# Turning the FFN product in 32x32 blocks on VectorE and through a DRAM buffer, instead of on TensorE

## The reference

```python
def swiglu(h, w_gate, w_up, w_down):          # h [256, 1024]
    return (jax.nn.silu(h @ w_gate) * (h @ w_up)) @ w_down   # w_gate, w_up [1024, 2816], w_down [2816, 1024]

x = x + 0.5 * swiglu(rms_norm(x, g[0]), ...)   # four times in the first two layers
x = x + (silu(gate) * up) @ w_down             # once in the hybrid layer
```

## Time and profile before

| | |
|---|---|
| time, median of 3 runs | 1378.87 us (1378.53 to 1378.92) |
| time of the profiled execution | 1378.48 us |
| its span, first to last instruction | 1376.7 us |
| PE busy | 1341.6 us (97% of the span) |
| DVE busy | 796.8 us (58%) |
| ACT busy | 645.7 us (47%) |
| POOL busy | 82.2 us (6%) |
| moved by DMA | 233.32 MB, mean 169 GB/s |
| granted clock of TensorE, mean | 0.996 of full |

### The profile page before, as it was taken

How to read it: one execution, slowest core, us unless ns; L and a number is a source line. 1 busy time by engine, 2 the same in 40 slices (tenths; PEclk the granted TensorE clock), 3 DMA queues, 4 the chain that set the end, 5 groups by cost and what they waited for, 6 DMA issues and landing times.

```text
span 1376.7 us, 17712 instructions
## 1 busy us (share of the span) xinstructions
PE 1341.6 (97%) x6710; PEld 1114.1 (81%) x6710; DVE 796.8 (58%) x873; ACT 645.7 (47%) x742; POOL 82.2 (6%) x181
## 2 busy tenths in 40 slices
PE   8999999999999999999999999999999998999998
PEld 7888889877888887788888877888887986788886
DVE  5555459746545545654556876544556887555444
ACT  5444457324444445544444856444445655444442
POOL 2000003100000001200000300000001200000000
PEclk9999999999999999999999999999999999999999
DMA  8655555414655554455553514655543452565551
GB/s 256 218 190 183 183 168 184 153 62 150 219 190 194 186 183 153 155 190 191 192 188 113 193 61 160 201 185 191 191 164 138 156 184 63 175 204 183 183 191 54
DMA packets 159326, 233.32 MB, mean 169 GB/s; under 512 B 7608, under 2 KB 126542, under 8 KB 159278
## 3 DMA queue, kind: packets, MB, share of 16 engines
q1 hardware_dynamic: 156560, 229.17, 50.5%
q10 hardware_dynamic: 2238, 2.70, 0.6%
q0 software_dynamic: 480, 0.80, 0.4%
HBM read 231.58 MB, written 1.05 MB: 169 GB/s over the span
## 4 chain that ended last, share of the span: by engine, by line
PE 92%; DVE 4%; ACT 2%; issue 1%; DMA 0%; POOL 0%; ACTq 0%; DVEq 0%; POOLq 0%
PE ps L250 27%; PE ps L252 26%; PE ps L251 26%; PE ps L545 2%; DVE wl L222 1%; PE ps L1012 1%; PE ps L266 1%; PE ps L334 1%; PE ps L268 1%; PE ps L267 1%; DVE htl L367 1%; PE ps L1526 1%; PE ps L1525 1%; ACT wh L211 1%; ACT hth L354 0%
## 5 line engine op out<-in xcount | busy, mean ns | idle before, releaser
L250 PE MATMUL ps<-wl,hth 128*128 128x512 f32 (+2 forms) x1280 | 504.6, 394 | 14.5 <-DVE htl L367 5.8
L252 PE MATMUL ps<-wh,htl 128*128 128x512 f32 (+2 forms) x1280 | 494.7, 386 | 0.0
L251 PE MATMUL ps<-wh,hth 128*128 128x512 f32 (+2 forms) x1280 | 493.9, 386 | 0.0
L714 DVE TENSOR_TENSOR wl<-raw,wh 128x2048 fp32r<-128x2048 f32 x120 | 275.1, 2292 | 204.9 <-ACT wh L663 204.9
L250 PEld LDWEIGHTS ps<-wl,hth 128*128 128x128 f32 x1280 | 240.5, 188 | 65.0 <-issue 15.2
L663 ACT ACTIVATE wh<-raw 128x2048 fp32r<-128x2048 f32 x120 | 229.7, 1914 | 123.6 <-PE ps L252 123.6
L252 PEld LDWEIGHTS ps<-wh,htl 128*128 128x128 f32 x1280 | 240.3, 188 | 49.3
L251 PEld LDWEIGHTS ps<-wh,hth 128*128 128x128 f32 x1280 | 240.8, 188 | 44.6
L222 DVE TENSOR_TENSOR wl<-raw,wh 128x2048 fp32r<-128x2048 f32 (+3 forms) x98 | 217.1, 2223 | 79.5 <-ACT wh L211 79.3
L211 ACT ACTIVATE wh<-raw 128x2048 fp32r<-128x2048 f32 (+3 forms) x98 | 181.0, 1853 | 65.7 <-PE ps L252 45.5
L250 PE MATMUL ps<-wl,prod_h 128*128 128x512 f32 x400 | 156.1, 390 | 0.0
(11 more groups left out here) (377 smaller groups left out, 990.7 us busy)
## 6 DMA issues: line engine op xcount, KB each, us to landing
raw<-in_ffn_w_down SPq DMA_DIRECT2D x88, 512.0 KB, 4.0
raw<-in_ffn_w_gate SPq DMA_DIRECT2D x86, 512.0 KB, 4.0
raw<-in_ffn_w_up SPq DMA_DIRECT2D x86, 512.0 KB, 4.9
raw<-in_w_gate_up SPq DMA_DIRECT2D x44, 512.0 KB, 4.7
raw<-in_even_w_in SPq DMA_DIRECT2D x24, 512.0 KB, 4.6
raw<-in_w_down SPq DMA_DIRECT2D x22, 512.0 KB, 3.6
raw<-in_ple_w_gate SPq DMA_DIRECT2D x16, 512.0 KB, 4.1
raw<-in_w_in SPq DMA_DIRECT2D x16, 512.0 KB, 4.4
```

Source lines behind the costliest of these rows:

```text
L250: nc.tensor.matmul(o, xh, b, start=first, stop=False)
L251: nc.tensor.matmul(o, xh, a, start=False, stop=False)
L252: return nc.tensor.matmul(o, xl, a, start=False, stop=last)
L714: nc.vector.tensor_tensor(wl[:, r, :], raw[:, r, :], wh[:, r, :].bitcast(f32), ALU.subtract)\
```

## The change

For chunks 1 to 9 of each FFN the four PE transposes, PSUM bank 2 between them and their readers, and the semaphore `prod_turned` are gone. In their place:

- DVE turns `prod` in blocks of 32x32, right behind the multiply (`turn_blocks`, one instruction of 512 elements per partition), into the first 512 columns of `xn[:, 0]`. It reads `prod` with a stride of 4 elements.
- ACT issues a DMA of these 128 x 512 floats (256 KB, one run of 2 KB per partition) to a DRAM buffer `bounce` (`move_out`), waits until it has landed, and issues a second DMA that reads it back into `xn[:, 1]` with the rows permuted, 512 runs of 512 bytes (`move_in`). With both, hidden features are on partitions.
- ACT's `high` and DVE's `low` read the moved data in SBUF, and not a PSUM bank. They stand one turn later, behind split 1 of the next turn.

Chunks 0 and 10 are still turned on PE. The halves of `prod_h` and `prod_l` are laid out token tile first, for all chunks.

```diff
+        prod_blocks = xn[:, 0, 0:512]
+        bounce = nc.dram_tensor("bounce", [P, 512], f32).ap()
+        prod_moved = xn[:, 1, 0:512]
+        moved_tiles = prod_moved.rearrange("p (q g t) -> p g q t", q=4, g=4)
...
@@ ffn_pe, in chunk(c) and before the loop
                 pe.wait_ge(prod_ready, c + (f * NCH + 1))
-                turn_product()
@@ ffn_act
+            def move_out(c):
+                act.wait_ge(blocks_ready, c + f * (NCH - 2))
+                act.dma_start(bounce, prod_blocks).then_inc(blocks_out, 16)
+
+            def move_in(c):
+                act.wait_ge(blocks_out, c * 16 + f * (NCH - 2) * 16)
+                act.dma_start(prod_moved.rearrange("p (q c) -> p q c", q=4),
+                              bounce.rearrange("(q n) (r c) -> (n r) q c", q=4, r=4)).then_inc(blocks_moved, 16)
+
+            def high(c):
+                act.wait_ge(blocks_moved, c * 16 + f * (NCH - 2) * 16)
+                nc.scalar.activation(prod_tiles(prod_h), moved_tiles, ACT.Copy).then_inc(prod_high, 1)
...
-            high(1)
+            move_out(1)
             with act.Fori(2, NCH - 1) as c:
+                move_in(c - 1)
                 split(c, 1)
+                high(c - 1)
                 split(c, 2)
                 silu(c * 3 + (n + 1))
                 split(c, 3)
-                high(c)
+                move_out(c)
             act_ahead.n += 3 * (NCH - 3)
+            move_in(NCH - 2)
+            act_ahead.through(act, n + FFN_SLOTS - 2)
+            high(NCH - 2)
@@ ffn_dve
+            def turn_blocks(c):
+                dve.wait_ge(prod_ready, c + (f * NCH + 1))
+                nc.vector.transpose(prod_blocks.rearrange("p (r g t) -> p g r t", r=4, g=4),
+                                    prod[:, :, :].rearrange("p t (k n r) -> p (t k) r n", k=2, r=4)).then_inc(blocks_ready, 1)
...
             with dve.Fori(2, NCH - 1) as c:
                 split(c, 1)
+                low(c - 1)
                 split(c, 2)
                 multiply(c)
+                turn_blocks(c)
                 split(c, 3)
-                low(c)
```

More of the change, by code:

```diff
@@ L151, in build_block @@
         prod_turned = sem("prod_turned")
+        blocks_ready = sem("blocks_ready")
+        blocks_out = sem("blocks_out")
+        blocks_moved = sem("blocks_moved")
         prod_high = sem("prod_high")
@@ L514, in ffn_load, with prod_tiles @@
             load_slot(sp, n + FFN_SLOTS - 1, down(n + FFN_SLOTS - 1, 2 * (NCH - 1)))
+        def prod_tiles(v):
+            return v[:, :, :].rearrange("p t (k q m) -> p (t k) q m", k=2, q=4)
         def ffn_pe(pe, n, s, f):
@@ L529, in down @@
                     at = kk * D + half * 512
-                    m = product(bank(4 + 2 * tt + half), h[:, kk, tt * P:(tt + 1) * P], l[:, kk, tt * P:(tt + 1) * P],
+                    m = product(bank(4 + 2 * tt + half), h[:, tt, kk * P:(kk + 1) * P], l[:, tt, kk * P:(kk + 1) * P],
                                 wh[:, place % RING, at:at + 512], wl[:, place % RING, at:at + 512],
@@ L541, in turn_product @@
             def turn_product(b=2):
-                for kk in range(2):
-                    for tt in range(TT):
-                        at = kk * T + tt * P
+                for tt in range(TT):
+                    for kk in range(2):
+                        at = tt * HC + kk * P
                         m = nc.tensor.transpose(ps[:, b, at:at + P], prod[:, tt, kk * P:(kk + 1) * P], ident[:, :])
@@ L650, in silu, with high_turned @@
                     nc.scalar.activation(silu_g[:, tt, :], ps[:, b + tt, 0:HC], ACT.Silu, scale=rstd[:, tt:tt + 1]).then_inc(silu_ready, 1)
-            def high(c, b=2, to=prod_h):
-                act.wait_ge(prod_turned, c + (f * NCH + 1))
-                nc.scalar.activation(to[:, :, :], bank(b).rearrange("p (k t) -> p k t", k=2), ACT.Copy)\
+            def move_out(c):
[8 more added lines that the diff above has]
+                nc.scalar.activation(prod_tiles(prod_h), moved_tiles, ACT.Copy).then_inc(prod_high, 1)
+            def high_turned(i, b, to):
+                act.wait_ge(prod_turned, 2 * f + i)
+                nc.scalar.activation(to[:, :, :], bank(b).rearrange("p (t k) -> p t k", t=TT), ACT.Copy)\
                   .then_inc(prod_high, 1)
@@ L674, in ffn_act @@
             act_ahead.through(act, n + 4)
-            high(0, 0)
+            high_turned(1, 0, prod_h)
             act_ahead.through(act, n + 5)
@@ L689, in ffn_act @@
             act_ahead.through(act, n + FFN_SLOTS)
-            high(NCH - 1, to=last_h)
+            high_turned(2, 2, last_h)
             if s + 1 in ple_of:
@@ L702, in multiply, with low, low_turned @@
                 m.then_inc(prod_ready, 1)
-            def low(c, b=2, to=prod_l, high=prod_h):
-                dve.wait_ge(prod_high, c + (f * NCH + 1))
-                nc.vector.tensor_tensor(to[:, :, :], bank(b).rearrange("p (k t) -> p k t", k=2),
+            def turn_blocks(c):
+                dve.wait_ge(prod_ready, c + (f * NCH + 1))
+                nc.vector.transpose(prod_blocks.rearrange("p (r g t) -> p g r t", r=4, g=4),
+                                    prod[:, :, :].rearrange("p t (k n r) -> p (t k) r n", k=2, r=4)).then_inc(blocks_ready, 1)
+            def low(c):
+                dve.wait_ge(prod_high, c + (f * NCH + 1))
+                nc.vector.tensor_tensor(prod_tiles(prod_l), moved_tiles, prod_tiles(prod_h).bitcast(f32),
+                                        ALU.subtract).then_inc(prod_low, 1)
+            def low_turned(c, b, to, high):
+                dve.wait_ge(prod_high, c + (f * NCH + 1))
+                nc.vector.tensor_tensor(to[:, :, :], bank(b).rearrange("p (t k) -> p t k", t=TT),
                                         high[:, :, :].bitcast(f32), ALU.subtract).then_inc(prod_low, 1)
@@ L724, in ffn_dve @@
             dve_ahead.through(dve, n + 4)
-            low(0, 0)
+            low_turned(0, 0, prod_l, prod_h)
             dve_ahead.through(dve, n + 5)
             multiply(1, 2)
+            turn_blocks(1)
             dve_ahead.through(dve, n + 6)
-            low(1)
             with dve.Fori(2, NCH - 1) as c:
                 split(c, 1)
+                low(c - 1)
                 split(c, 2)
                 multiply(c)
+                turn_blocks(c)
                 split(c, 3)
-                low(c)
             dve_ahead.n += 3 * (NCH - 3)
+            dve_ahead.through(dve, n + FFN_SLOTS - 2)
+            low(NCH - 2)
             dve_ahead.through(dve, n + FFN_SLOTS - 1)
@@ L739, in ffn_dve @@
             dve_ahead.through(dve, n + FFN_SLOTS)
-            low(NCH - 1, to=last_l, high=last_h)
+            low_turned(NCH - 1, 2, last_l, last_h)
             if s + 1 in ple_of:
```

1 line of the change is left out of this document (removed).

## The result

The changed kernel takes 1356.62 us (median of 4 runs), the kernel before 1378.7 in the same measurement: a ratio of 0.9844, 95% interval 0.9832 to 0.9856. Forecast were 1358.0 us and a range of 1356.2 to 1364.0. The profiled execution took 1356.98 us with a span of 1355.2, 21.5 us less than the span before.

The account below looks back on a forecast made before the run. PE, busy 97% of the span, was taken as the bound. Removing 45 transpose groups at 0.46 us saves 20.7 us, additions cost nothing: 1378.48 - 20.7 = 1357.8, given as 1358.0 us; 8-in-10 range 1356.2 to 1364.

Parts of the forecast that it names:

- Price of a group: Four PE transposes of one chunk cost 0.46 us; removing 45 groups saves 20.7 us.
- its two prices: For a transpose group: 0.45 us from matmul start distances, 0.47 us from the loop turn's balance; together 20.3 to 21.2 us.
- Block transpose: New DVE step behind the multiply: 0.69 us, upper bound 2.29, off the path; 31 us of DVE time over all.
- Landings: Store to DRAM taken to land in 3.0 us, permuted read back in 4.5 us, both hidden under PE.
- D: Sum of the store's and read back's landings, taken as 7.5 us; PE stays the bound up to 9.7.
- two of its own signs: Expected in the profile after: store landing within 3.5 us; ACT's high starting within 5.5 us of the turn's start.
- signs of being wrong: PE idle before down matmuls ended by prod_l, or before a turn's first matmul; silu late, with ACT awaiting the landing.
- High and low: ACT's high 0.60 us, DVE's low 0.69 us, read from SBUF; prod_low ready 4.5 us before the down product.
- The lap: Ring from one move_out to the next: 6.6 us plus landings, 14.1 against PE's 16.34; rival that it sets pace 0.08.
- Loop's end: Rival: at the loop branch PE shows a bubble of about 0.45 us, time stays 1378 to 1380; chance 0.03.
- Traffic: 90 added transfers, 24 MB on 233; gate and up loads keep a cover of 6 us, so nothing reaches the path.
- The slow read: Rival: permuted read back 19 times slower, 42 us, kernel 1575 us slower, 2950 in all; chance 0.01.

Follow-up runs that it names:

- e8: Kernel before, with the four PE transposes of chunks 1 to 9 made twice into the same bank: 1399.11 us, ratio 1.0149.
- e6: Changed kernel with other block transpose patterns: contiguous reads in FFN 0, contiguous writes in FFN 1, both in FFN 2: 1356.38 us, one execution.
- e3: Changed kernel with one more 256 KB DRAM-to-DRAM transfer, waited for, between store and read back: 1452.96 us, ratio 1.0534.
- e4: Changed kernel with two more 256 KB DRAM-to-DRAM transfers, each waited for, between store and read back: 1592.63 us, a single execution.
- e9: Changed kernel with the block transpose made twice by VectorE, the first into a buffer nobody reads: 1357.72 us, ratio 0.9849.
- e2: Kernel before, all transposes kept, with block transpose, store, read back and a ScalarE pass added, result unused: 1378.69 us, ratio 0.9997.

## Why the prediction was right, step by step

*Price of a group.* Taken 0.46 us, measured 0.48 (16.80 to 16.32 us a turn). The higher of its two prices, from the turn's own balance, was nearly right; the distance over three instructions stopped too early, since the next matmuls behind the transposes (at 60.66, 60.90, 61.13 us, one turn ahead of the earlier trace rows) are still 0.24 and 0.23 us apart and not 0.2267, which adds some 0.03 us. The sum was 20.7 us; the span fell by 21.5. The lower end of the forecast's own range has a slip: with a group at 0.48 us the time is 1378.48 - 21.6 = 1356.9 us and not 1356.5. e8 confirms the price from the other side, with 20.3 us for 180 more.

*Block transpose.* Taken 0.69, measured 1.12 us; the bound of 2.29 held. The step that failed was "the count of elements is the same": the read takes every fourth element, and e6 shows that this costs 0.41 us. DVE gained 49 busy us and not 31. It cost PE nothing, since the multiply's end and split 3 had the room the prediction named.

*Landings.* Taken 3.0 and 4.5, measured 2.5 and 5.0, so D = 7.5 as taken; that the sum came out exactly is luck, as each landing was off by 0.5 us and the two errors cancel. In the first FFN they are 3.6 and 5.1, and D = 8.7. The prediction took one D for all turns, and two of its own signs fail there: the store lands later than 3.5 us, and `high` starts 6.4 us after the turn and not within 5.5, so that split 2 starts at 7.0 us and not at 5.7. None of its signs of being wrong appears: PE never waits for `prod_l`, and silu waits for PE.

*High and low* were taken at 0.60 and 0.69 and took 0.63 and 0.69. `prod_low` was forecast 4.5 us ahead of the down product. In FFN 1 the turn with `high` at 409.25 has `low` done at 410.60 and the down product at 415.14, 4.5 us; in the first FFN it is 3.1.

```profile
409.91 0.69 DVE L740 TENSOR_TENSOR prod_l<-xn,prod_h 128x512 fp32r<-128x512 f32 x1 [0.84 <-ACT prod_h L673]
...
415.14 0.39 PE L257 MATMUL ps<-wl,prod_h 128*128 128x512 f32 x1
```

*The lap* was the right thing to watch: by its law, with the landings of those runs, e3 and e4 should turn in 18.8 and 21.8 us, and they take 18.59 and 21.67. The turning point D = 10.2, where the turn is as long as before, is with the slower block transpose 9.8. What the prediction missed is that D is not a number that one may add to: it depends on when in the turn the store and the read back are issued. e9 added 1.1 us and got it back from the landings outside the first FFN.

*Loop's end.* The rival of a bubble is out: matmuls run at 0.227 us across the branch, with the wait for `prod_ready` on the register instruction. Of the stall that the Trainium skill (Runtime: NRT & Kernel Launch, "Instruction fetch mechanics") describes for a branch whose target isn't fetched, no run here shows anything.

*Traffic.* 24 MB more delayed the up loads by 0.1 us, and e2 prices the whole trip at nothing, 0.9997.

*The slow read.* The factor of 19 did not appear: 256 KB in runs of 512 bytes landed in 5.0 us beside a pair of weight loads and in 2.8 ahead of one. The estimate by the Trainium skill (DMA: Bandwidth & Descriptors, "Anatomy of one DMA"), 2.6 us a trip, is nearly met by the read back in e9 (2.8) and undercut by the store there (2.0); beside other loads it is too low by half (5.0). The page's fit is for transfers issued by GpSimd, and these were issued by ACT, so here it is an estimate only.

## What to carry to other kernels

Where PE is the bound and the other engines wait for it, small PE work between matmuls is worth its start-to-start distance, and a detour through VectorE and two DMAs of some 9 us can replace half a microsecond of PE, if it closes within a turn. Draw the lap that the detour closes through in-order engines, with all that stands on it, and compare it with the turn; the slack at the consumer is not enough. And look at what is in the DMA queues at the moment of issue: the same 256 KB read took 2.8 or 5.0 us by being issued just before or with a pair of weight loads. A measurement of the moment alone, with all else equal, was not made.

## What the runs showed of the hardware that was not expected

**Landing by moment of issue.** The 256 KB store landed in 4.5 us when issued 1.3 us after the second load of a weight pair (e3), in 3.6 at about 2 us after it (first FFN of the changed kernel), and in medians of 2.5 and 2.0 over all turns, most of them issued about 3 and 4 us after it (other FFNs, e9).

**The clock when PE waits.** In e3 and e4 PE waits for `prod_low`, 58.7 us in 40 waits and 141.5 us in 44, and the mean granted clock of TensorE fell to 0.978 and 0.933, against 0.997 in the changed kernel. In one turn of e3 (93.0 to 111.6 us) it was 0.91. PE had waited 1.91 us before the down product at 93.43; for 3 us after it the clock is at its lower level, 1.2 GHz, as this one of them shows (PE, PEld, DVE, ACT and POOL busy, then the granted clock):

```profile
95.00:96.00 1.00, 1.00 (x3) 0.73 (x3) 1.00 (x3) 0.66 (x1) 0.00 (x0) 0.50 0.87 332
```

There matmuls are 0.43 us apart and not 0.227. By the next turn's wait of 0.20 us the clock did not fall.

The scatter of both kernels goes with the clock too: executions of the changed kernel with a mean of 0.997 took 1355.96 to 1356.98 us, those with 0.993 took 1359.84 and 1359.9; the kernel before took 1381.8 to 1382.4 at 0.993 and 1377.6 to 1379.9 above it. Two executions of the changed kernel, the repeated one (1358.51 us) and the first (1356.98), differ in this window of a `ple` stage, in which PE is busy for only some 3 of 5 us (columns as above); first the repeated one:

```profile
1165.00:1170.00 5.00, 3.02 (x8) 2.43 (x9) 3.86 (x5) 1.57 (x4) 0.00 (x0) 0.66 0.27 105
```

```profile
1165.00:1170.00 5.00, 3.21 (x16) 2.69 (x17) 3.86 (x5) 1.46 (x4) 0.00 (x0) 1.00 0.27 105
```

The clock was granted at 0.66 on average in the one and in full in the other, after the same pause of PE, 2.77 us. A mean of 0.66 over 5 us is an estimated loss of 5 x 0.34 = 1.7 us, and the two executions are 1.5 us apart. Those at 1359.8 and 1359.9 us were not profiled, so that such stretches make up their excess too is not shown, and why the same pause lowers the clock in one execution and not in the other stays open.
